# Shifting the moving weights by 32 and 96 bytes, where they stood 64 bytes over a multiple of 128

## What is computed

```python
# layer 1: attention and a linear recurrence, then a gated FFN
mix = concatenate([attn, lru]) @ w_out            # (256,1024) @ (1024,1024)
ffn = (gelu(c_g) * c_u) @ w_down                  # (256,2816) @ (2816,1024)
# layer 2: neighbourhood attention, then SwiGLU
m = o @ na_w_o                                    # (256,1024) @ (1024,1024)
f = (silu(gate) * up) @ ffn_w_down                # (256,2816) @ (2816,1024)
# layer 3: latent attention, then 8 experts, two for each token
m = o @ mla_w_o
for e in range(8):
    gate, up = split(hf @ w_gu[e])                # (., 1024) @ (1024, 3584)
    y = y + combine[:, e] * ((silu(gate) * up) @ w_down[e])   # (., 1792) @ (1792, 1024)
```

## Time and profile before

| | |
|---|---|
| median of three runs | 1271.77 us (1268.66 to 1274.67) |
| the profiled execution | 1269.44 us, of which the span of its instructions is 1267.5 us |
| TensorE clock granted | 0.997 of full on the mean |
| TensorE busy | 1221.6 us of the span |
| bytes from and to memory | 369.09 MB, 291 GB/s on the mean |

### The profile page before, as it was taken

One profiled execution on the slowest core, in us unless ns is written; L12 is line 12 of the kernel. 1 busy time (PEld: TensorE's weight loads), 2 busy tenths in 40 slices (PEclk: granted clock), 3 DMA queues, 4 the chain that ended last, 5 costly groups with the idle time before them and its releaser, 6 DMA issues.

```text
span 1267.5 us, 20171 instructions
## 1 busy us (share of the span) xinstructions
PE 1221.6 (96%) x7626; PEld 1080.1 (85%) x7626; DVE 1021.1 (81%) x1099; ACT 782.0 (62%) x997; POOL 94.1 (7%) x111
## 2 busy tenths in 40 slices
PE   6989999999999999999999999999999999999995
PEld 5978999977888799998897778898989898989884
DVE  6887899996755578777756578989898989898987
ACT  5774666544555454443346656777777777777764
POOL 0020000000572100000002202000000000000020
PEclk9999999999999999999999999999999999999998
DMA  9963897679933559988973239999999999999991
GB/s 314 353 225 100 311 332 264 243 298 252 259 119 128 207 210 334 332 323 308 387 259 120 77 113 400 399 396 351 401 356 397 349 398 350 409 342 410 341 411 69
DMA packets 163838, 369.09 MB, mean 291 GB/s; under 512 B 24404, under 2 KB 96415, under 8 KB 157367
## 3 DMA queue, kind: packets, MB, share of 16 engines
q1 hardware_dynamic: 157201, 350.72, 77.7%
q10 hardware_dynamic: 5094, 12.11, 2.6%
q0 software_dynamic: 1472, 5.28, 1.1%
HBM read 360.72 MB, written 14.70 MB: 296 GB/s over the span
## 4 chain that ended last, share of the span: by engine, by line
PE 74%; DVE 14%; ACT 4%; issue 3%; DMA 2%; POOL 2%; ACTq 0%; DVEq 0%; SPq 0%
PE ps L1340 20%; PE ps L1367 11%; PE ps L808 5%; PE ps L810 5%; PE ps L809 5%; PE ps L820 5%; PE ps L822 5%; PE ps L824 5%; DVE wlo L1919 3%; PE ps L880 2%; DVE cv L2260 2%; PE ps L872 2%; DMA raw<-in_moe_w_gu 2%; DVE wlo L1927 2%; POOL probs L2663 1%
## 5 line engine op out<-in xcount | busy, mean ns | idle before, releaser
L1405 ACT ACTIVATE whi<-raw 128x1024 fp32r<-128x1024 f32 x190 | 195.9, 1057 | 145.8 <-PE ps L810 88.9
L1919 DVE TENSOR_TENSOR wlo<-raw,whi 128x1024 fp32r<-128x1024 f32 x190 | 231.6, 1248 | 64.3 <-ACT whi L1405 61.1
L808 PE MATMUL ps<-ahi,whi 128*128 128x256 f32 x864 | 242.6, 281 | 2.7 <-DVE alo L1952 2.4
L809 PE MATMUL ps<-alo,whi 128*128 128x256 f32 x864 | 239.9, 278 | 0.0
L810 PE MATMUL ps<-ahi,wlo 128*128 128x256 f32 x864 | 239.9, 278 | 0.0
L1927 DVE TENSOR_TENSOR wlo<-raw,whi 128x1792 fp32r<-128x1792 f32 (+1 forms) x96 | 199.2, 2088 | 25.5 <-ACT whi L1419 25.1
L1419 ACT ACTIVATE whi<-raw 128x1792 fp32r<-128x1792 f32 (+1 forms) x96 | 167.2, 1755 | 56.7 <-PE ps L1340 25.7
L808 PEld LDWEIGHTS ps<-ahi,whi 128*128 128x128 f32 x864 | 163.1, 189 | 5.1 <-issue 4.2
L809 PEld LDWEIGHTS ps<-alo,whi 128*128 128x128 f32 x864 | 163.0, 189 | 0.7 <-issue 0.7
L810 PEld LDWEIGHTS ps<-ahi,wlo 128*128 128x128 f32 x864 | 162.8, 188 | 0.0
L1340 PE MATMUL ps<-whi,hchi 128*128 128x448 f32 x352 | 102.1, 371 | 2.9 <-DVE wlo L1927 1.6
(11 more groups left out here) (351 smaller groups left out, 2405.1 us busy)
## 6 DMA issues: line engine op xcount, KB each, us to landing
raw<-in_moe_w_gu SPq DMA_DIRECT2D x96, 896.0 KB, 7.0
ada<-in_w_ada SPq DMA_DIRECT2D x48, 1024.0 KB, 7.3
raw<-in_moe_w_down SPq DMA_DIRECT2D x32, 1024.0 KB, 7.8
ada<-in_moe_w_gu SPq DMA_DIRECT2D x32, 896.0 KB, 7.3
raw<-in_w_up SPq DMA_DIRECT2D x22, 1024.0 KB, 6.6
raw<-in_ffn_w_gu SPq DMA_DIRECT2D x22, 1024.0 KB, 8.9
ada<-in_moe_w_down SPq DMA_DIRECT2D x16, 1024.0 KB, 9.1
raw<-in_na_w_qkv SPq DMA_DIRECT2D x12, 1024.0 KB, 8.5
```

The lines of the kernel that those rows point to most:

```text
L808: pe.matmul(o, h[:, k, cols], bhi[:, k], start=(k == 0), stop=False)
L809: pe.matmul(o, h[:, k, cols], blo[:, k], start=False, stop=False)
L1405: act.activation(high_, src, ACT.Copy).then_inc(hi_done, 1)
L1919: ve.tensor_tensor(low_, src, high_.bitcast(F32), ALU.subtract).then_inc(lo_done, 1)
```

## The change

The place where a moving weight chunk begins depends on the product, no longer on the slot alone.

- First layer's `w_out` and `w_down`, and the experts' gate and up: 32 bytes (8 elements) over a multiple of 128.
- Second layer's `na_w_o` and `ffn_w_down`, third layer's `mla_w_o`, the experts' down: 96 bytes (24 elements).
- The value projections of layers 1 and 2 keep 64 bytes, the chunk in `ghi` keeps 0. The values' half of `mla_w_ukv` goes from 64 to 0.
- The third place is given its own tiles, `third_hi` and `third_lo`, which lie over `ahi` and `alo` from 64 bytes ahead of them.
- `same` compares `moved` where it compared `by_rows`: for the chunk in `ghi` it is now false.

```diff
-        whi = [whi2[:, s] for s in range(NSPLIT)] + [ahi_flat]
-        wlo = [wlo2[:, s] for s in range(NSPLIT)] + [alo_flat]
+        whi = [whi2[:, s] for s in range(NSPLIT)] + [at("third_hi", CHUNK + HALF_LINE * 3 // 2, F32R, offset=ahi_at - HALF_LINE * 4)]
+        wlo = [wlo2[:, s] for s in range(NSPLIT)] + [at("third_lo", CHUNK + HALF_LINE * 3 // 2, F32R, offset=alo_at - HALF_LINE * 4)]
...
-        moved_at = [HALF_LINE, HALF_LINE, 0, 0]
-        def by_rows(c):
-            if W_QKV <= c < W_NAO:
-                return QKV_ORDER[c - W_QKV][1] == 2
-            return W_IN + 8 <= c < W_UP or W_DOWN <= c < W_QKV or W_NAO <= c < W_GU or W_DN2 <= c < W_MDN or W_MLO <= c < W_MOE
+        def moved(c):
+            if c in OVER_GATED:
+                return 0
+            if c in (W_IN + 8, W_IN + 9) or W_QKV <= c < W_NAO and QKV_ORDER[c - W_QKV][1] == 2:
+                return HALF_LINE
+            if W_OUT <= c < W_UP or W_DOWN <= c < W_QKV:
+                return HALF_LINE // 2
+            return HALF_LINE * 3 // 2 if W_NAO <= c < W_GU or W_DN2 <= c < W_MDN or W_MLO <= c < W_MOE else 0
...
-        def split_of_expert(ck):
-            n = moved_at[ck.half]
+        def split_of_expert(ck, c):
+            n = HALF_LINE // 2 if c % PASS_CHUNKS < 16 else HALF_LINE * 3 // 2
             return [w[ck.half][:, n:n + CHUNK] for w in (whi, wlo)]
...
-            n = D + moved_at[half]
-            return [w[half][:, n:n + D] for w in (whi, wlo)]
+            return [w[half][:, D:2 * D] for w in (whi, wlo)]
...
-                same = ck.mate is None or (chunk_shape(c), by_rows(c)) == (chunk_shape(ck.mate), by_rows(ck.mate))
+                same = ck.mate is None or (chunk_shape(c), moved(c)) == (chunk_shape(ck.mate), moved(ck.mate))
```

More of the change, by code:

```diff
@@ L530, in expert_shape @@
             return (2, EH) if c < 16 else (1, D) if c in (16, PASS_CHUNKS - 1) else (2, D)
-        moved_at = [HALF_LINE, HALF_LINE, 0, 0]
-        def by_rows(c):
-            if W_QKV <= c < W_NAO:
-                return QKV_ORDER[c - W_QKV][1] == 2
-            return W_IN + 8 <= c < W_UP or W_DOWN <= c < W_QKV or W_NAO <= c < W_GU or W_DN2 <= c < W_MDN or W_MLO <= c < W_MOE
+        def moved(c):
[6 more added lines that the diff above has]
+            return HALF_LINE * 3 // 2 if W_NAO <= c < W_GU or W_DN2 <= c < W_MDN or W_MLO <= c < W_MOE else 0
         def split_of(c):
-            half = Chunk(c).half
-            n = moved_at[half] if by_rows(c) else 0
+            half, n = Chunk(c).half, moved(c)
             return [w[half][:, n:n + CHUNK] for w in (whi, wlo)]
-        def split_of_expert(ck):
-            n = moved_at[ck.half]
+        def split_of_expert(ck, c):
+            n = HALF_LINE // 2 if c % PASS_CHUNKS < 16 else HALF_LINE * 3 // 2
             return [w[ck.half][:, n:n + CHUNK] for w in (whi, wlo)]
@@ L1334, in expert_pass @@
                                 pe.wait_ge(sem("hc_ready"), 1 + q // 2 + 2 * p)
-                            h, l = (view(w, 2, EH) for w in split_of_expert(ck))
+                            h, l = (view(w, 2, EH) for w in split_of_expert(ck, 8 * j + 4 * part + q))
                             for k in range(2):
@@ L1362, in expert_pass @@
                     ck = begin_expert(c, p)
-                    h, l = (view(w, kc, D) for w in split_of_expert(ck))
+                    h, l = (view(w, kc, D) for w in split_of_expert(ck, c))
                     for k in range(kc):
@@ L1417, in split_expert @@
                 k, n = expert_shape(c)
-                high_, _ = split_of_expert(ck)
+                high_, _ = split_of_expert(ck, c)
                 act.activation(high_[:, 0:k * n], raws[ck.slot][:, 0:k * n], ACT.Copy).then_inc(moe_hi, 1)
@@ L1925, in split_expert @@
                 k, n = expert_shape(c)
-                high_, low_ = split_of_expert(ck)
+                high_, low_ = split_of_expert(ck, c)
                 ve.tensor_tensor(low_[:, 0:k * n], raws[ck.slot][:, 0:k * n], high_[:, 0:k * n].bitcast(F32), ALU.subtract)\
```

## The result

| | before | after |
|---|---|---|
| median | 1269.85 us (10 runs, 1267.7 to 1274.67) | 1273.4 us (10 runs, 1271.44 to 1276.19) |
| ratio | | 1.0026, 95% interval 1.0015 to 1.0038 |
| span of the profiled execution | 1267.5 us | 1270.1 us |

The kernel became slower by 3.3 us (0.0026 x 1269.85). That is less than the half per cent that I had named as what a measurement of this kernel can tell from no change, but ten runs of each tell it. I had forecast 1.3 us less. This ratio and the later ones, with their 95% intervals, are taken over the runs of both kernels; they are not the quotients of the two medians, from which they differ by up to 0.0007.

The account below looks back on a forecast made before the run. It took TensorE's matmul spacing to set the time. Between 7.4 us gained and 4.9 lost it took the middle, -1.3 us: 1269.4 to 1268.1 profiled, 1271.8 to 1270.5 on the median; forecast's range 1267 to 1275, whole range 1262 to 1277.

Parts of the forecast that it names:

- which stretches set the time: Middle of `w_down`, `ffn_w_down` and whole expert passes: TensorE has practically no idle time; in the last pass gains only partly return.
- the costs put at nothing: Splits writing at 32 or 96 bytes (uncovered 5.1 us), the `ghi` chunk's wait (uncovered 2.75 us, twice), values under 0.1 us.
- DMA would not come into the passes: Expert passes: 404 against 375 GB/s leaves 7%; the rival that DMA takes the gain back had chance 0.02, no change.
- My rival with no effect of the start: All by-rows products: the halves differ as regions 8320 bytes apart, so nothing moves; 1271.8 us, chance 0.20.
- the bounds: By-rows matmuls all at the best level shown, 227.5 and 200.0 ns, or all at the worst, 233.3 and 203.3.
- the step between the bounds: Straight lines over distance gave -0.8 us for experts' down, -0.1 for `ffn_w_down`; the bounds' middle, -1.3 us, was taken.
- Distance 32, half 0: `w_down`, gate and up: 32 lies between 227.5 and 229.2 ns, so `w_down` stays; gate and up had no line.
- Distance 96, half 0: `ffn_w_down` and experts' down: between 229.2 and about 233 ns, a loss of 1.8 ns a matmul.
- Distance 224, half 1 and third place: `ffn_w_down` and experts' down: between 232.9 and 227.5 ns, a gain of 2.7 ns a matmul.
- Distance 160: Half 1 and third place of `w_down`, gate and up: near 233 ns with 512 columns, so `w_down` stays.
- The raster rival: All by-rows matmuls: starts off multiples of 64 bytes cost 3.7 or 3.3 ns more, 9.4 us together, 1281.2; chance 0.13.
- Theory D: From the experiments, not the prediction: by-rows matmul cost depends only on moving operand's distance behind the stationary tile, modulo 256 bytes.

Follow-up runs that it names:

- all starts back: The changed kernel with all moving starts of the products by rows back at 64 bytes, the rest of the change kept; 1270.03 us against 1270.3, ratio 1.0005.
- the run with both sides moved: The changed kernel with the experts' stationary tiles put 224 bytes further on, weights still on odd multiples of 32; ratio 1.0007 to the kernel before.
- the shift of either side: Stationary tiles moved 128 bytes in the kernel before, weights unmoved: ratio 0.9992; moving starts were shifted by the change itself: ratio 1.0026.
- the second set of starts: The changed kernel with longer third-place tiles and another start for each of 24 expert chunks, so other chunks had the first set's distances; one run, 1276.08 us.

## Why the prediction was wrong

**Right:** which stretches set the time; that little but the distance between matmul starts would change (a wait of 1.22 us in `w_down` became 1.50); the costs put at nothing (the wait of the chunk in `ghi` and the values, since with all starts back the loss was gone; the splits, since ScalarE needs 1062 ns in `w_down` before and after and is busy for 782.0 and 782.1 us); that DMA would not come into the passes; that the distance to the stationary tile is what orders the levels where it is a multiple of 64. My rival with no effect of the start falls.

**Right by luck:** the bounds, 7.4 us gained and 4.9 lost, held the 3.3 lost, but the upper one rests on no level going over 233.3 and 203.3 ns, and 233.9, 234.2 and 205.1 did; other places came out under their bound and made up for it. In `ffn_w_down` the two halves did draw nearer to each other, because the good one got worse. And the time of 1273.4 us lies inside the forecast's own range of 1267 to 1275; that range stood around a median of three runs, 1271.77, which ten runs put at 1269.85.

**Wrong:** the step between the bounds. I took the levels for a function that runs straight between its rows at 0, 64 and 192, and then, since these lines alone came to some 0.8 us gained, the middle of the bounds, -1.3 us, which no mechanism gives. Term by term, as expected and as measured:

- Distance 32, half 0: I had `w_down` stay near 229 and gate and up unchanged. Measured 233.4 ns with 512 columns and 205.1 with 448, 4.0 and 4.4 ns more.
- Distance 96, half 0: I had 1.8 ns more. Measured 4.5, 233.9.
- Distance 224, half 1 and third place: I had 2.7 ns less. Measured 233.1, nothing less. This was the term that gave the forecast its sign.
- Distance 160: I had no change. Measured 234.2 with 512 columns, 1.1 more, and 201.6 with 448, 0.7 less.

A slip without weight: the bounds count the 288 matmuls of the output projections at distances 64 and 192, though with `ahi` as stationary operand they stood at 0 and 128. Counted rightly each bound moves by some 0.1 us.

So with 512 columns 0 and 64 are both good (228.9 and 229.4 ns), and 32, between them, is not (233.4). A line drawn between two good levels was a bad level's estimate. The raster rival, which I gave 0.13, had the sign, and in half 0 it had the size (3.7 and 3.3 ns expected, 4.0 to 4.5 measured). Its sign of 5.6 us and more for both halves of `w_down` came true (5.61 and 5.62), that of passes over 62 us did not (61.66). It was wrong in charging half 1 and the third place too, which made 9.4 us of what became 3.3, and wrong in its cause: the run with both sides moved shows that starts off the raster are as fast as others when the distance is a multiple of 64.

The sign that I had named, chunks 4 and 5 at 5.50 and 5.59 us to within 0.03, failed at chunk 4 with 5.61. So did the one that the level would stay between 227.5 and 233.3, with 233.9 and 234.2.

**Open:** why these distances, and why at 32 and 160 one distance has several levels (last section). That the moving read and the weight load meet at the same memory at the same time would explain why their distance counts, and the shift of either side agrees with it. No run took the load away or moved it in time, so it is argued and not shown. The Trainium skill, "TensorE: Matmul & The Clock Gate", section "Step-by-step: what each phase is for", gives the two operands independent read ports; these runs show that the time depends on both addresses together nevertheless.

## What to carry to other kernels

Where a weight tile is the moving operand and each matmul brings a new stationary tile, the place of one behind the other, modulo 256 bytes, was worth 2 to 7 ns of each matmul of 448 or 512 columns here. Read it from the distances between starts, by buffer, before touching anything: two slots with different levels in the kernel before were a gain in plain view, and giving all three places of the experts the better one's distance, and the down products too, was worth 2.3 us, where shifting both by 32 bytes cost 3.3. Don't interpolate between measured distances; put a different start into each chunk of a loop and read the levels from the profile, chunk by chunk and pass by pass, since a distance may have more than one. Of the distances tried, 64 was the safe one: 200 or 201 ns in every chunk with 448 columns, in the kernel with all three places there.

## What the runs showed of the hardware that I had not expected

**One distance can have several levels, and a chunk keeps to one.** In the kernel with gate and up at 32 in all places, chunk 10 (half 0) of three passes takes 2.40, 2.46 and 2.48 us for its twelve matmuls, at the same addresses in the same execution. The rows are the first matmuls of chunks 10 and 11:

```profile
905.40 0.36 PE L1338 MATMUL ps<-whi,hchi 128*128 128x448 f32 x1
...
907.80 0.36 PE L1338 MATMUL ps<-third_hi,hchi 128*128 128x448 f32 x1
...
1028.60 0.37 PE L1338 MATMUL ps<-whi,hchi 128*128 128x448 f32 x1
...
1031.06 0.37 PE L1338 MATMUL ps<-third_hi,hchi 128*128 128x448 f32 x1
...
1090.46 0.37 PE L1338 MATMUL ps<-whi,hchi 128*128 128x448 f32 x1
...
1092.94 0.37 PE L1338 MATMUL ps<-third_hi,hchi 128*128 128x448 f32 x1
```

Within the first of these chunks every distance between starts is 200 ns; in the second they go from 202 to 206 (204.4 on the mean), in the third they are 206 and 207. Chunk 9 ahead of it has the same level each time. So the 203.9 ns above are a mean over three levels, 200.0, 204.4 and 206.7, the lowest of which is as good as distance 64. It is the same at 160: half 1 ran at 200.0 in most chunks of the changed kernel, at 206.7 in chunk 3 of four of its eight passes, and at 206.3 in the second set of starts. At 64, over all chunks of the kernel with all places there, the means of the chunks are 200 or 201 ns. What sends a chunk to one level or another no run shows. Theory D therefore holds where the distance is a multiple of 64; at 32 and 160 the distance alone does not give the cost.

**So can the form by columns.** In the gate and up of layer 2 the last two kernels run the same code on the same addresses. Windows of the two, wholly inside that stage, with the columns of the earlier trace rows; first the kernel with all places at 64:

```profile
480.00:550.00 70.00, 70.00 (x620) 70.00 (x619) 56.37 (x48) 34.65 (x40) 0.00 (x0) 1.00 0.96 326
```

and the one with gate and up of the experts at 32, which come later in the program:

```profile
480.00:550.00 70.00, 70.00 (x596) 70.00 (x596) 55.24 (x47) 32.85 (x38) 0.00 (x0) 1.00 0.91 311
```

The starts are 113.3 ns apart on the mean in one and 117.8 in the other, at the same granted clock. The stage has 960 such matmuls and takes 108.8 us (from 464.0 to 572.7) in one and 113.0 (from 461.1 to 574.2) in the other, 4.2 us between two executions, as much as the whole effect studied here. The nine other profiles, in whose kernels half 1 lies 128 bytes elsewhere, have 113.4 to 113.7 ns in these 70 us. I have one profile of each of the two and can't say how often either level occurs, or whether it is behind the 5 to 9 us between the fastest and the slowest run of a kernel.
